# Both feed-forward stages rewritten in two phases by one level of Strassen's scheme

## The reference

```python
h = h + 0.5 * _swiglu(_rms_norm(h, ffn1_norm[l]), ffn1_w_gate[l], ffn1_w_up[l], ffn1_w_down[l])
...
h = h + merged @ w_mix_out[l]
h = h + _cross_attention(_rms_norm(h, xattn_norm[l]), _rms_norm(mem, mem_norm[l]), w_q[l], w_kv[l], w_xo[l])
h = h + 0.5 * _swiglu(_rms_norm(h, ffn2_norm[l]), ffn2_w_gate[l], ffn2_w_up[l], ffn2_w_down[l])
return _rms_norm(h, final_norm)
```

## Time and profile before

| what | us |
|---|---|
| median of 3 runs (lowest, highest) | 2351.93 (2347.86, 2354.65) |
| profiled execution, first to last instruction (span) | 2353.6 |
| PE busy in it | 2235.3 |
| DVE, POOL, ACT busy in it | 1060.9, 810.7, 280.1 |

### The profile page before, as it was taken

How to read it: one execution, slowest core, us unless ns; L and a number is a source line. 1 busy time by engine, 2 the same in 40 slices (tenths; PEclk the granted TensorE clock), 3 DMA queues, 4 the chain that set the end, 5 groups by cost and what they waited for, 6 DMA issues and landing times.

```text
span 2353.6 us, 25297 instructions
## 1 busy us (share of the span) xinstructions
PE 2235.3 (95%) x10082; PEld 1850.8 (79%) x10082; DVE 1060.9 (45%) x1133; ACT 280.1 (12%) x326; POOL 810.7 (34%) x601
## 2 busy tenths in 40 slices
PE   4699999999999999899998999899999999999995
PEld 4577888888888877777887888788888888888884
DVE  7976333233333277754434265425332333333336
ACT  1032000000000020001112123302000000000001
POOL 4743333333333332212332431133333333333330
PEclk9799999999999999999999999999999999999997
DMA  5343111111111116232112141211111111111111
GB/s 193 104 165 99 54 45 46 52 45 51 38 53 53 45 45 172 68 101 76 45 53 108 45 161 54 90 54 45 45 54 45 53 45 45 53 45 45 44 45 72
DMA packets 67195, 161.89 MB, mean 69 GB/s; under 512 B 6977, under 2 KB 32321, under 8 KB 66113
## 3 DMA queue, kind: packets, MB, share of 16 engines
q1 hardware_dynamic: 29232, 106.97, 13.7%
q10 hardware_dynamic: 37904, 54.09, 7.0%
HBM read 135.36 MB, written 26.72 MB: 69 GB/s over the span
## 4 chain that ended last, share of the span: by engine, by line
PE 87%; DVE 10%; issue 1%; ACT 1%; DMA 1%; POOL 0%; ACTq 0%; POOLq 0%; DVEq 0%
PE ps L300 86%; DVE prep L932 3%; DVE ua_lo L932 1%; DVE prep L941 1%; PE ps L365 0%; DVE h L941 0%; DMA d_kv_lo<-kv_lo 0%; ACT ua_hi L617 0%; DVE mx_a L932 0%; DVE mx_b L932 0%; DMA eye<-in_eye 0%; DVE mx_pooled L932 0%; DVE s_perm L932 0%; DVE kv_lo L932 0%; DVE pt_lo L932 0%
## 5 line engine op out<-in xcount | busy, mean ns | idle before, releaser
L277 POOL TENSOR_TENSOR w_lo<-raw,w_hi 128x1024 fp32r<-128x1024 f32 x202 | 552.4, 2735 | 16.9
L273 POOL TENSOR_TENSOR tick<-tick 128x1 f32<-128x1 f32 x192 | 51.8, 270 | 1414.8 <-PE ps L300 1411.9
L300 PE MATMUL ps<-ua_hi,w_hi 128*128 128x512 f32 x1312 | 516.8, 394 | 15.1 <-DVE ua_lo L932 7.1
L300 PE MATMUL ps<-ua_lo,w_hi 128*128 128x512 f32 x1312 | 514.5, 392 | 0.0
L300 PE MATMUL ps<-ua_hi,w_lo 128*128 128x512 f32 x1312 | 406.3, 391 | 0.0
L1185 DVE SCALAR_TENSOR_TENSOR h<-ps,h 128x1024 f32<-128x1024 f32 x192 | 235.2, 1225 | 296.5 <-PE ps L300 278.0
L300 PE MATMUL ps<-ub_hi,w_hi 128*128 128x512 f32 x832 | 323.9, 389 | 0.0
L300 PE MATMUL ps<-ub_lo,w_hi 128*128 128x512 f32 x832 | 323.8, 389 | 0.0
L300 PEld LDWEIGHTS ps<-ua_hi,w_hi 128*128 128x128 f32 x1312 | 249.1, 190 | 71.8 <-issue 8.9
L300 PEld LDWEIGHTS ps<-ua_lo,w_hi 128*128 128x128 f32 x1312 | 248.9, 190 | 51.3
L300 PEld LDWEIGHTS ps<-ua_hi,w_lo 128*128 128x128 f32 x1312 | 248.1, 189 | 52.2
(11 more groups left out here) (200 smaller groups left out, 2301.5 us busy)
## 6 DMA issues: line engine op xcount, KB each, us to landing
raw<-in_weights SPq DMA_DIRECT2D x202, 512.0 KB, 3.5
d_h<-h ACTq DMA_DIRECT2D x16, 512.0 KB, 5.0
h<-d_h ACTq DMA_DIRECT2D x16, 512.0 KB, 7.1
h<-in_x ACTq DMA_DIRECT2D x8, 512.0 KB, 9.4
out<-h ACTq DMA_DIRECT2D x8, 512.0 KB, 2.7
d_f<-prep ACTq DMA_DIRECT2D x1, 2304.0 KB, 16.7
d_kv_hi<-kv_hi ACTq DMA_DIRECT2D x2, 1024.0 KB, 5.2
d_kv_lo<-kv_lo ACTq DMA_DIRECT2D x2, 1024.0 KB, 8.4
```

What stands on the lines that cost most here:

```text
L273: nc.gpsimd.tensor_tensor(tick[:, 1:2], tick[:, 0:1], tick[:, 0:1], op=ALU.add)
L277: nc.gpsimd.tensor_tensor(lo, raw[:, k % RAW, :], hi.bitcast(F32), op=ALU.subtract).then_inc(s_w_split, 1)
L300: ins = nc.tensor.matmul(out, lhsT, rhs, start=start, stop=stop)
```

## The change

Each feed-forward is now done in two phases: all gate and up products first, then all down products. Both are cut into 2 x 2 blocks and multiplied by one level of the Strassen-Winograd scheme: 7 block products in place of 8. The blocks go by parity: even and odd tiles of the inner and the outer dimension, and the two halves of 512 tokens. So each operand needs sums of blocks. For the weights POOL makes the sums (`total`) and the low halves (`low`), and ACT the high halves (`block_high`). For the input of gate and up, DVE makes the sums once, at the start of a stage (`x_sums`). For the input of down, DVE makes them step by step (`act_sum`, `act_low`). DVE combines the block results out of PSUM (`add`, `evacuate`).

Gate and up: 22 products (n) of 7 passes of 12 matmuls. Down: 7 products (s) of 11 steps of 12 matmuls; the table `DN` gives the weight blocks, the activation blocks and the targets of each. Weights are held in a ring of six half units. The hidden activations are stored to DRAM in the gate and up phase by SP and loaded back ahead of the down phase (`before_down`) into the space that the gate and up input leaves. The `tick` instruction, the loops and POOL's `w_hi` of feed-forward weights are gone. The tables of rotations (`rotation`) now stand in `h` for a while. The other stages compute what they did, with weights in the new ring. The last steps of the feed-forward finish the odd tiles of `h` first, and the mixer's opening takes them first.

```diff
+GU_ORDER = ("w11", "w12", "s2", "s1", "w22", "s3", "s4")
+GU_FIRST = ("s1", "s2", "s3", "w22", "w11", "w12", "s4")
+GU_X = {"w11": ("b", 0), "w12": ("b", 1), "s4": ("b", 2), "s1": ("t", 0), "s3": ("t", 1), "w22": ("t", 2), "s2": ("t", 3)}
+GU_N = 7 * FT
...
+DN = (((2, 3, 1), (0,), (((1, 0), 1), ((1, 1), -1))),
+      ((2, 0, -1), (0, 1, 1), (((1, 1), 1),)),
+      ((0,), (1, 3, -1), (((0, 1), 1), ((1, 1), 1))),
+      ((0, 3, 1), (0, 3, 1), (((0, 0), 1), ((1, 1), 1))),
+      ((3,), (2, 0, -1), (((0, 0), 1), ((1, 0), 1))),
+      ((0, 1, 1), (3,), (((0, 0), -1), ((0, 1), 1))),
+      ((1, 3, -1), (2, 3, 1), (((0, 0), 1),)))
...
-            def split(u, k, slot, wait_used=True):
-                pool.wait_ge(raw_landed[k % RAW], 16 * (k // RAW + 1) if u is None else (u * (16 // RAW) + 16 * (k // RAW + 1)))
-                if wait_used:
-                    pool.wait_ge(s_w_used, k - RING + 1 if u is None else u + (k - RING + 1))
-                if u is not None:
-
-                    nc.gpsimd.tensor_tensor(tick[:, 1:2], tick[:, 0:1], tick[:, 0:1], op=ALU.add)
-                hi, lo = w_hi[:, slot].rearrange("p k c -> p (k c)"), w_lo[:, slot].rearrange("p k c -> p (k c)")
-                nc.gpsimd.tensor_scalar(hi, raw[:, k % RAW, :], 1.0, 0.0, ALU.mult, ALU.add).then_inc(s_w_hi, 1)
-                pool.wait_ge(s_w_hi, k + 1 if u is None else u + (k + 1))
...
+                def gu_pass(op, bank, kp):
+                    side, x = GU_X[op.key[3]]
+                    xhi, xlo = ((xb_hi, xb_lo) if side == "b" else (xt_hi, xt_lo))
+                    xhi, xlo = xhi[:, x, kp], xlo[:, x, kp]
+                    h = op.halves[0]
+                    last = kp == KP - 1
+                    mm(bank, w_hi[:, h, kp], xhi, kp == 0, False)
+                    mm(bank, w_hi[:, h, kp], xlo, False, False)
+                    mm(bank, w_lo[:, h, kp], xhi, False, last, signal=s_gstep if last else None)
+
+                first = [next(passes) for _ in range(7)]
+                for part, ops in enumerate((first[:4], first[4:])):
+                    for kp in range(KP):
+                        if part == 0:
+                            pe.wait_ge(s_xt_lo, 2 * (KP * f + kp + 1))
+                        else:
+                            pe.wait_ge(s_xb_lo, 2 * (KP * f + kp + 1))
+                        for op in ops:
+                            if kp == 0:
+                                wait_bank("gu", 0, op.key[2])
+                                pe.wait_ge(s_w_low, op.low)
+                            gu_pass(op, ffn_bank(f, "gu", 0, op.key[2]), kp)
+
+                for n in range(1, FT):
+                    for i, name in enumerate(GU_ORDER):
+                        op = next(passes)
+                        if n == 1 and i == 1:
...
+                for s in range(len(DN)):
+                    for kp in range(FP):
+                        op, d = next(passes), s * FP + kp
+                        pe.wait_ge(s_w_low, op.low)
+                        pe.wait_ge(s_a_lo, DN_N * f + d + 1)
+                        ahi, alo = xt_hi[:, 3, d % 4], xt_lo[:, 3, d % 4]
+                        h = op.halves[0]
+                        for mp in range(MP):
+                            if kp == 0:
+                                wait_bank("dn", s, mp)
+                            bank = ffn_bank(f, "dn", s, mp)
+                            end = kp == FP - 1
+                            mm(bank, w_hi[:, h, mp], ahi, kp == 0, False)
+                            mm(bank, w_hi[:, h, mp], alo, False, False)
+                            mm(bank, w_lo[:, h, mp], ahi, False, end,
+                               signal=s_dbank if end else s_dstep if mp == MP - 1 else None)
...
+                if d == 15:
+                    sp.wait_ge(s_actst, 32 * FP * (f + 1))
+                    for b in (0, 1, 3, 2):
+                        act_load(b, 10, 11, s_acts_last[b])
...
+            def low(op, src):
+
+                h = op.halves[0]
+                hi, lo = (w[:, h].rearrange("p k c -> p (k c)") for w in (w_hi, w_lo))
+                pool.wait_ge(s_w_high, op.high)
+                add(lo, src, hi.bitcast(F32), op=ALU.subtract).then_inc(s_w_low, 1)
...
+                else:
+                    lower("w11")
+                    pool.wait_ge(s_w_low, by["w11"].low)
+                    pool.wait_ge(s_w_sum, n_sum)
+                    total(b[0], b[0], b[2])
+                    lower("w12")
+                    lower("s2")
+                    lower("s1")
+                    pool.wait_ge(s_w_low, by["s1"].low)
+                    pool.wait_ge(s_w_sum, n_sum + 1)
+                    total(b[2], b[0], b[3], ALU.subtract)
+                    pool.wait_ge(s_w_low, by["w12"].low)
+                    total(b[1], b[1], b[0])
+                    lower("w22")
+                    lower("s3")
+                    lower("s4")
+
+            def down(ops):
+                def total(op):
...
+            def down(ops):
+                def total(op):
+                    w = DN[op.key[1]][0]
+                    if len(w) > 1:
+                        landed(op)
+                        add(raw_part(op, 0), raw_part(op, 0), raw_part(op, 1),
+                            op=ALU.add if w[2] > 0 else ALU.subtract).then_inc(s_w_sum, 1)
+
+                total(ops[0])
+                for d, op in enumerate(ops):
+                    if d + 1 < len(ops):
+                        total(ops[d + 1])
+                    low(op, raw_part(op, 0))
...
+                splits("start")
+                for k in range(KP):
+                    for j in range(2):
+                        m = 2 * k + j
+                        act.wait_ge(s_tile, KT * f + m + 1)
+                        if k and j == 0:
+                            act.wait_ge(s_sqadd, (KT - 1) * f + m - 1)
+                        nc.scalar.activation(X[j][:], h[:, m], ACT.Copy, scale=gain(m)).then_inc(s_xf, 1)
+                        splits(("tile", m))
+                    if f == 0 and k == 0:
+                        act.wait_ge(s_kstore, 32)
+                        act.wait_ge(s_estore, 32)
+                        act.wait_ge(s_pstore, 16)
+                    for j in range(2):
+                        act.wait_ge(s_xd, 4 * (KP * f + k) + 2 * j + 2)
+                        nc.scalar.activation(xt_hi[:, 2 * j:2 * j + 2, k], two(X[j]), ACT.Copy).then_inc(s_xt_hi, 1)
+                    splits(("kp", k))
+                    if k < KP - 1:
+                        act.wait_ge(s_xt_lo, 2 * (KP * f + k + 1))
+                        square(2 * k, sq if k else acc)
...
+                    dve.wait_ge(s_xf, KT * f + 2 * k + 2)
+                    count = 4 * (KP * f + k)
+                    v.tensor_tensor(sq[:, C0], sq[:, C0], sq[:, C1], ALU.subtract).then_inc(s_xd, 1)
+                    dve.wait_ge(s_xd, count + 1)
+                    v.tensor_tensor(sq[:, C1], rn[:, C1], sq[:, C1], ALU.subtract).then_inc(s_xd, 1)
+                    dve.wait_ge(s_xd, count + 2)
+                    v.scalar_tensor_tensor(out=rn[:, C1], in0=sq[:, C0], scalar=-1.0, in1=rn[:, C1],
+                                           op0=ALU.mult, op1=ALU.subtract).then_inc(s_xd, 1)
+                    dve.wait_ge(s_xd, count + 3)
+                    v.scalar_tensor_tensor(out=rn[:, C0], in0=rn[:, C1], scalar=-1.0, in1=rn[:, C0],
+                                           op0=ALU.mult, op1=ALU.subtract).then_inc(s_xd, 1)
+
+                def x_sums_low(k):
+                    for j, x in enumerate((sq, rn)):
+                        dve.wait_ge(s_xt_hi, 2 * (KP * f + k) + j + 1)
+                        v.tensor_tensor(xt_lo[:, 2 * j:2 * j + 2, k], two(x[:]), xt_hi[:, 2 * j:2 * j + 2, k].bitcast(F32),
+                                        ALU.subtract).then_inc(s_xt_lo, 1)
+
+                def add_squares(m):
...
+            def act_sum(f, d):
+
+                s, k = d // FP, d % FP
+                y = DN[s][1]
+                if len(y) == 1:
+                    return
+                for b in y[:2]:
+                    wait_acts(dve, f, b, k)
+                dve.wait_ge(s_a_lo, DN_N * f + d - 1)
+                v.tensor_tensor(f_g[:, 0, (d % 2) * HALF:(d % 2 + 1) * HALF], acts_at(y[0], k), acts_at(y[1], k),
+                                ALU.add if y[2] > 0 else ALU.subtract).then_inc(s_a_sum, 1)
+
+            def act_low(f, d):
+                s, k = d // FP, d % FP
+                y = DN[s][1]
+                src = f_g[:, 0, (d % 2) * HALF:(d % 2 + 1) * HALF] if len(y) > 1 else acts_at(y[0], k)
+                if len(y) > 1:
+                    dve.wait_ge(s_a_sum, a_sums(f, d))
+                dve.wait_ge(s_a_hi, DN_N * f + d + 1)
+                v.tensor_tensor(xt_lo[:, 3, d % 4], src, xt_hi[:, 3, d % 4].bitcast(F32), ALU.subtract).then_inc(s_a_lo, 1)
+
+            def evacuate(f, s, mp):
+
+                dve.wait_ge(s_dbank, DN_BANKS * f + MP * s + mp + 1)
```

(85 more changed lines are left out.)

1950 lines of the change are left out of this document (1152 added, 798 removed).

## The result

The changed kernel takes 2366.86 us (median, 2361.89 to 2368.81) against 2352.01 us in the same comparison: a ratio of 1.0063, 95% interval 1.0049 to 1.0078. It is slower by some 15 us, where 60 us faster was forecast. Its profiled execution has a span of 2365.0 us.

What follows compares the result with a forecast made beforehand. PE, busy 95% of the span, was taken as the bound, so fewer matmuls pay at full pace. The sum was 2353.6 - 179.5 - 8 + 3 + 42 + 55 + 10 + 10 + 4 + 2 = 2292 us, range 2246 to 2365.

Steps and rivals of the forecast that it cites:

- the pace: PE's time per matmul, read in the down stage: 0.2267 us each, so 792 fewer matmuls give -179.5 us.
- Removed, other waits: The 2.75 us weight wait ahead of the last down pair and the slow clock behind it go, twice: -8 us.
- Lengths at 512 columns: Instruction times estimated for 512 columns: DVE 0.69 us, ACT 0.60, POOL 1.30 (bounds 1.13 and 1.47).
- Gate and up, steady: In gate and up PE stays the limit at 19.04 us a product; rotation tables in the first feed-forward add +3.
- rival C: POOL becomes the limit in gate and up too, products longer than 19.3 us: 2380 us, slower; chance 0.14.
- Down, steady: In down, steps with sums exceed PE's 2.72 us because POOL and DVE share a path: +23 and +19, +42 us.
- Rival B: The path shared by POOL and DVE gives no stall, down taking 210 us: 2247 us; chance 0.18.
- Rival D: Gaps in down steps drop PE's clock to 1.2 GHz for stretches: +65 us, 2357; chance 0.08.
- Start of the first: In the first feed-forward PE waits for input tiles and the seventh weight block; product 0 ends near 210: +55 us.
- The hand-over: Between gate and up and down, activation loads queue behind weights and the last store is late: +5 per feed-forward, +10 us.
- rival E: At the hand-over to down, reloads in one queue with weights come 15 us late each time: 2322 us; chance 0.10.
- The mixer's first unit and the tail: At the end of down POOL makes the mixer's first unit only then, +4 us; the last squares, +2.

Runs made afterwards that it cites:

- e1: The changed kernel with 32 bytes of unused space put back where `tick` stood; 2328.62 us, span 2325.4, ratio 0.9907 to the kernel before.
- e7: e1 with POOL's sums of weight blocks left out in the down phase; 2279.55 us, span 2279.2.
- e8: e1 with DVE's sums of activation blocks left out in the down phase; 2284.19 us, span 2281.6.
- e5: e1 with DVE's five bank-freeing additions of the first product put ahead of the norm factor's chain; 2312.6 us, span 2307.2.
- e6: e1 with reloads of two activation blocks issued behind the last tile's store and reload; 2318.0 us, span 2315.9.
- e10: e1 with the orders of e5 and e6, plus the second activation block's first megabyte issued behind weights of down steps 4 to 7; 2306.85 us, span 2302.9.
- e4: The kernel before with `tick` made 32 bytes longer, nothing else; 2402.2 us, ratio 1.0223 to the kernel before.

## Why the prediction was wrong

*The step that failed* is the pace, "so 0.2267 us each", carried over to all matmuls that remain. The removed matmuls are worth 179.5 us as said, but of the 9290 others the 8372 with 512 columns went to 0.2334. By e1 that is 39.6 us, of the 73 us between forecast (2292) and span (2365.0). The forecast has no term for the removal of `tick`: it used the instruction, 0.20 us on POOL, only for a length, and its 32 bytes of place were not weighed at all. Had they been, the rest comes to 2325, faster, and 33 us from the number.

*Removed, other waits* (-8): the kernel before spent 12.6 and 7.1 us over pace in its feed-forwards (730.8 and 725.3 us for 3168 matmuls), so -20: 12 us better than forecast. (The window from 840 to 845 holds the wait of 2.75 us itself; the 1.3 us taken for the slow clock stand even so: it reads 0.50 from 843.4 to 846.)

*Lengths at 512 columns*: right. POOL 1.29 for 1.30, DVE 0.68 for 0.69, ACT 0.60 to 0.63 for 0.60. The estimate of 1.12 us from the Trainium skill's GPSIMD Engine Reference, section 3.1, does not hold here: the same rows read 1.29 alone, and the down phase cost what 1.30 had given.

*Gate and up, steady*: right, 19.04 us a product in e1, to the last digit; the rotations cost nothing (+3 forecast). In the changed kernel itself a product takes 19.60 us, over the 19.3 that was named as the sign of rival C, POOL as the limit. But e1 brings 19.04 back with POOL's work untouched, so the sign came from the address and C did not.

*Down, steady* (+42): right in mechanism and size. e1 shows 26 and 19 us over pace for 23 and 19, and e7 and e8 take away all but 1 to 2 of it. The weight-sum steps of the sixth product, forecast at 3.05 us, kept 2.72; the last product alone loses 13.8 and 7.0 of the 26 and 19. Rival B is refuted by the same runs. Rival D, a slow clock through the down steps for +65, did not come: the granted clock is 1.00 in e1's window from 700 to 800 and 0.96 from 800 to 877. It was low only at the hand-over, 0.80 from 623 to 670, where PE waited in pieces.

*Start of the first* (+55) came out at 51, *of the second* (+10) at 9. The order of waits that was followed is the one in the timeline; the wait for the seventh block, forecast at 8 us or so in both, was 2.4 and 5.1.

*What the forecast didn't have* is the second product and what trails it in the third: 14 to 16 us in each feed-forward, 29 in all. It stopped its walk through the waits at the end of product 0, where DVE's queue held the norm factor ahead of the additions that free the banks. e5 gets 18 of them back.

*The hand-over* (+10) measured 41: a term mis-sized, and rival E's place. The forecast named the queue order and the late last store, but counted 3.5 MB ahead of it. In the profile 40 us run at 332 to 360 GB/s with a DMA share near 1: all four blocks (11.5 MB) and weights of up to two blocks per step. e6 shows that the order is worth 10 us, e10 that one more change of order is worth nothing. In e7 the first down product takes 46 us in place of 51 and 50, so POOL's sums have 4 to 5 us in each. That the rest is the bytes fits the full DMA engines, but no run took bytes away.

*The mixer's first unit and the tail* (+6): the stages between took 725.9 us in e1 and 734.1 before, so -8 where +4 stood; the tail 3.4 more, where +2 stood. Why the stages between gained was not tried. PE's waits there are as long in both, 31 us in all; the granted clock is 0.97 before and 0.99 in e1, and of the 2719 matmuls of 512 columns 45 go at 0.43 us before and 24 in e1. That is some 4 of the 8 us; the rest, and what held the clock up, stay open.

Together, against the forecast: 40 (pace) + 29 (second product) + 31 (hand-over) + 3 (down) - 5 (starts) - 3 (rotations) - 12 (mixer) + 1 (tail) - 12 (waits of before) = 72, of the 73. So the 33 us that remain beside the pace are no measure of how good the other terms were: terms that were 64 us too small and others that were 32 too large half cancel, and that is luck.

## What to carry to other kernels

Before believing a matmul count, compare PE's time per matmul in a stage that was not changed. If it differs while the clock reads the same, look at where the buffers lie: any tensor added or removed moves all that follow, and here 32 bytes were worth 40 us by spans in one kernel (e1) and 45 in the other (e4). Where a phase shares a path between two engines, taking one instruction from either is worth the same. When an order of waits is followed, follow it until PE runs freely for good, and give each transfer burst its bytes by the measured rate.
